# A decoder block with 16,384 single-neuron experts: one gather for each chosen expert, against every expert for every token with one-hot gates

## The reference, cut to what matters

```python
D_MODEL, SEQ = 1024, 1024                 # BATCH = 1, DEPTH = 1
N_KEYS, PEER_HEADS, PEER_TOPK = 128, 8, 16
N_EXPERTS = N_KEYS * N_KEYS

def reference(x, ...):
    h = rmsnorm(x, mix_norm_g)
    q, k, v, gb, gc, hc = split(h @ w_in, 6)
    mixed = concat(rmsnorm(stick_breaking_attention(q, k, v)),
                   rmsnorm(short_gated_conv(gb, gc, hc)))
    x = x + mixed @ w_out
    xn = rmsnorm(x, ffn_norm_g)
    x = x + peer(xn, peer_wq, peer_keys, peer_u, peer_v)
    return rmsnorm(x, final_norm_g)

def peer_chunk(xc, wq, keys, u_tab, v_tab):       # 128 tokens
    q = (xc @ wq).reshape(128, PEER_HEADS, 256)
    s1 = einsum('thd,hnd->thn', q[..., :128], keys[0])
    s2 = einsum('thd,hnd->thn', q[..., 128:], keys[1])
    v1, i1 = top_k(s1, 16); v2, i2 = top_k(s2, 16)
    best, pos = top_k(v1[..., :, None] + v2[..., None, :], 16)   # over 256 pairs
    idx = (i1 * N_KEYS + i2) at pos
    g = softmax(best)
    act = gelu(einsum('td,thkd->thk', xc, u_tab[idx]))
    return einsum('thk,thkd->td', g * act, v_tab[idx])
```

## Time and profile before

| | us |
|---|---|
| median of 3 runs | 3488.6 |
| range | 3485.1 to 3492.64 |
| the profiled execution | 3493.22 |
| its span, first to last instruction | 3491.5 |

### The profile page before, as it was taken

One profiled execution on the slowest core, in us unless ns is written; L12 is line 12 of the kernel. 1 busy time (PEld: TensorE's weight loads), 2 busy tenths in 40 slices (PEclk: granted clock), 3 DMA queues, 4 the chain that ended last, 5 costly groups with the idle time before them and its releaser, 6 DMA issues.

```text
span 3491.5 us, 29071 instructions
## 1 busy us (share of the span) xinstructions
PE 2454.5 (70%) x7552; PEld 1321.4 (38%) x7552; DVE 2663.4 (76%) x6520; ACT 687.7 (20%) x1947; POOL 1382.3 (40%) x1296
## 2 busy tenths in 40 slices
PE   8569895589989785675878787576667555554554
PEld 7447463246545342223544333243223222211221
DVE  1674689865778799897779788689877577777776
ACT  2122311121434111112114332111111111111111
POOL 0132323333334333444445445344444344444442
PEclk9779998899999897887889899898788777777777
DMA  6878697789888998889999999999888899999997
GB/s 217 313 299 325 266 381 292 292 334 356 331 330 329 380 355 311 325 339 368 415 411 377 341 370 388 387 394 371 334 356 340 337 374 380 380 370 372 380 383 293
DMA packets 185037, 1212.83 MB, mean 347 GB/s; under 512 B 20672, under 2 KB 20672, under 8 KB 53440
## 3 DMA queue, kind: packets, MB, share of 16 engines
q0 software_dynamic: 147456, 1073.81, 78.7%
q1 hardware_dynamic: 37440, 137.40, 10.4%
HBM read 1198.54 MB, written 12.58 MB: 347 GB/s over the span
## 4 chain that ended last, share of the span: by engine, by line
PE 34%; DVE 29%; DMA 23%; ACT 6%; issue 5%; POOL 2%; POOLq 0%; DVEq 0%; ACTq 0%; SPq 0%
DMA ring<-in_uv,cur_idx 22%; PE vacc L900 17%; DVE ring L1075 11%; PE bank L938 6%; DVE acc L1106 4%; ACT diag L731 3%; PE bank L1006 3%; PE o_ps L904 2%; POOL ring L694 2%; DMA xn<-in_final_norm_g 1%; PE bank L934 1%; DVE lt L1223 1%; DVE ocT L1233 1%; PE bank L949 1%; PE bank L967 1%
## 5 line engine op out<-in xcount | busy, mean ns | idle before, releaser
L900 PE MATMUL vacc<-ring,diag 128*128 128x512 f32 x2048 | 1267.1, 763 | 985.5 <-ACT diag L731 983.2
L694 POOL DMA_INDIRECT ring<-in_uv,cur_idx x1024 | 1215.1, 1187 | 1172.5 <-PE vacc L900 611.6
L1075 DVE CUSTOM_DVE_ANT_0 ring<-ring,xn 128x1024 f32<-128x1024 f32 x1024 | 1219.5, 1222 | 351.6 <-DMA ring<-in_uv,cur_idx 349.0
L900 PEld LDWEIGHTS vacc<-ring,diag 128*128 128x128 f32 x2048 | 481.7, 246 | 1670.2 <-ACT diag L731 1027.2
L1106 DVE SCALAR_TENSOR_TENSOR acc<-ring,g_w,acc 128x512 f32<-128x512 f32 x832 | 625.6, 752 | 35.2 <-DVE g_w L1098 0.6
L685 POOL COPY cur_idx<-idx 128x4 uint32<-128x4 uint32 (+1 forms) x256 | 165.2, 645 | 904.9 <-DVE acc L1106 693.6
L726 ACT ACTIVATE g_ex<-g_cu 128x4 f32<-128x4 f32 x256 | 52.4, 205 | 2071.6 <-DVE g_cu L1088 2055.3
L731 ACT ACTIVATE diag<-ident,g_w 128x128 f32<-128x128 f32 x1024 | 326.8, 390 | 187.8 <-DVE g_w L1098 184.5
L938 PE MATMUL bank<-hT,wpool 128*128 128x256 f32 (+2 forms) x1280 | 285.0, 382 | 1.4 <-ACT hT L757 1.4
L938 PEld LDWEIGHTS bank<-hT,wpool 128*128 128x128 f32 x1280 | 219.8, 192 | 69.1 <-issue 12.1
L1017 PE MATMUL bank<-hT,wpool 128*128 128x256 f32 (+2 forms) x1024 | 235.9, 386 | 0.7 <-ACT hT L839 0.7
(11 more groups left out here) (126 smaller groups left out, 1798.2 us busy)
## 6 DMA issues: line engine op xcount, KB each, us to landing
wpool<-in_w_in SPq DMA_DIRECT2D x96, 512.0 KB
wpool<-in_peer_wq SPq DMA_DIRECT2D x64, 512.0 KB
wpool<-in_w_out SPq DMA_DIRECT2D x32, 512.0 KB
ring<-in_uv,cur_idx POOLq DMA_INDIRECT x1024
xb<-in_x SPq DMA_DIRECT2D x15, 512.0 KB
x_scratch<-xb SPq DMA_DIRECT2D x8, 512.0 KB
xn_scratch<-xb SPq DMA_DIRECT2D x8, 512.0 KB
xn<-xn_scratch SPq DMA_DIRECT2D x8, 512.0 KB
```

The lines of the kernel that those rows point to most:

```text
L694: nc.gpsimd.indirect_dma_start(ring[:, s, :], None, uv, bass.IndirectOffsetOnAxis(ap=cur_idx[:, s:s + 1], axis=0))\
L900: ins = nc.tensor.matmul(vacc[:, :], diag[:, q, s, :], ring[:, q * GROUP + s, D:D + PE_COLS], start=first and s == 0, stop=last and s == G ...
L1075: ins = nc.vector.tensor_tensor_reduce(out=ring[:, s, 0:D], in0=ring[:, s, 0:D], in1=xn[:, c % 2, :], scale=1.0, scalar=0.0, op0=ALU.mult, ...
```

## The change

The front keeps its mathematics. The gathers, the ring and the body are gone. In their place all 16,384 experts are applied to all tokens, in 128 tiles of 128 experts (tile a holds the experts whose first key is a), and a **pass** over all tiles is made for each 256 tokens. That is 4 passes x 128 = 512 tiles.

- For one tile n, `up` is eight 128x256 products (L836), `down` four 128x512 products (L848) that accumulate in four PSUM banks over the pass.
- The gates of a tile (128 experts by 256 tokens) are zero but for the chosen experts. They are built by `scatter`: for each token, a 128x128 one-hot matrix of its slots' second keys (`one_b`, DVE L1105, bare ones) times a 128x64 matrix that holds the gate where the slot's first key matches (`one_a`, DVE L1113). Four tokens make a step (four products with a 64-wide moving tile, L824), 64 steps cover 64 first keys for 256 tokens (a range), and ACT copies them out of PSUM into `gates` (L638).
- The gates are built a range, 64 tiles, ahead: at tile n the step n+64 is made. The first 64 steps stand before tile 0, and the last 64 tiles have none.
- The gelu of a tile goes from ACT (Square, L656) to DVE (L1148) to ACT (Tanh, L658) to DVE (L1153), then DVE multiplies with the gates (L1160).
- Each tile loads 512 KB of u and 512 KB of v by plain DMAs of SP, with three slots for each.
- The front is in four batches of two chunks. `front_line()` lays the projections of one batch beside the attention of the batch before and the search of the one before that, in six rounds. The dense part starts when the whole front is over (`front_over`). Results of the search are transposed into `selT`.

The core of the diff (of the front only its order; all lines here are new, in place of `timeline`, of the groups and of `final_sum` and its like):

```diff
-BATCHES = [[0], [1, 2], [3, 4, 5], [6, 7]]
+BATCHES = [[0, 1], [2, 3], [4, 5], [6, 7]]
+PASSES = S // T
+TILES = PASSES * NKEYS
+RANGE = 64
+SCAT_TOK = T // RANGE
+USLOTS = 3
+VSLOTS = 3
+HBUF = 4
...
+def front_line():
+    out = []
+    for r in range(len(BATCHES) + 2):
+        lists = []
+        for stage, make in enumerate((proj_steps, mix_steps, find_steps)):
+            if 0 <= r - stage < len(BATCHES):
+                lists.append(make(r - stage))
+        marked = [((i + 0.5) / len(ls), n, i) for n, ls in enumerate(lists) for i in range(len(ls))]
+        for _, n, i in sorted(marked):
+            out += lists[n][i]
+    return out
...
+            front_over(sp)
+            for n in range(TILES):
+                if n >= USLOTS:
+                    sp.wait_ge(s_up, n - USLOTS + 1)
+                sp.dma_start(u_in[:, n % USLOTS, :], ut[n % NKEYS]).then_inc(s_uin[n % USLOTS], 16)
+                if n >= VSLOTS:
+                    sp.wait_ge(s_vp, n - VSLOTS + 1)
+                sp.dma_start(v_in[:, n % VSLOTS, :], vt[n % NKEYS]).then_inc(s_vin[n % VSLOTS], 16)
...
+            for n in range(TILES):
+                act.wait_ge(s_up, n + 1)
+                if n >= HBUF:
+                    act.wait_ge(s_vp, n - HBUF + 1)
+                nc.scalar.activation(hid[:, n % HBUF, :], u_ps[n % 2][:, 0:T], ACT.Square).then_inc(s_hsq, 1)
+                act.wait_ge(s_hcu, n + 1)
+                nc.scalar.activation(hid[:, n % HBUF, :], hid[:, n % HBUF, :], ACT.Tanh,
+                                     scale=GELU_TANH * GELU_CUBE).then_inc(s_hth, 1)
+                if n % 2 and n + RANGE < TILES:
+                    store_gates((n + RANGE) // 2)
...
+            def scatter(s):
+                q = s // 2
+                pe.wait_ge(s_one, s + 1)
+                if s % 2 == 0 and q >= 2:
+                    pe.wait_ge(s_gates, q - 1)
+                for j in range(SCAT_TOK):
+                    o = ((s % 2) * SCAT_TOK + j) * RANGE
+                    ins = nc.tensor.matmul(sc_ps[q % 2][:, o:o + RANGE], one_b[:, s % 2, j, :], one_a[:, s % 2, j, :],
+                                           start=True, stop=True, skip_group_check=True)
+                ins.then_inc(s_scat, 1)
...
+            def up(n):
...
+                pe.wait_ge(s_uin[n % USLOTS], 16 * (n // USLOTS + 1))
+                if n >= 2:
+                    pe.wait_ge(s_hgl, n - 1)
+                for k in range(KD):
+                    ins = nc.tensor.matmul(u_ps[n % 2][:, 0:T], u_in[:, n % USLOTS, k * P:(k + 1) * P],
+                                           xT[:, p % 2, k * T:(k + 1) * T], start=k == 0, stop=k == KD - 1)
+                ins.then_inc(s_up, 1)
+
+            def down(n):
...
+                pe.wait_ge(s_vin[n % VSLOTS], 16 * (n // VSLOTS + 1))
+                pe.wait_ge(s_hw, n + 1)
...
+            front_over(pe)
+            for s in range(RANGE):
+                scatter(s)
+            for n in range(TILES):
+                up(n)
+                if n + RANGE < TILES:
+                    scatter(n + RANGE)
+                if n > 0:
+                    down(n - 1)
+            down(TILES - 1)
...
+            for s in range(RANGE):
+                ones_b(s)
+                ones_a(s)
+            for n in range(TILES):
+                h = hid[:, n % HBUF, :]
+                u = u_ps[n % 2][:, 0:T]
+                r = n // RANGE
+                dve.wait_ge(s_hsq, n + 1)
+                nc.vector.scalar_tensor_tensor(out=h, in0=h, scalar=1.0 / GELU_CUBE, in1=u, op0=ALU.add,
+                                               op1=ALU.mult).then_inc(s_hcu, 1)
+                if n + RANGE < TILES:
+                    ones_b(n + RANGE)
+                dve.wait_ge(s_hth, n + 1)
+                nc.vector.scalar_tensor_tensor(out=h, in0=h, scalar=1.0, in1=u, op0=ALU.add, op1=ALU.mult)\
+                    .then_inc(s_hgl, 1)
+                if n + RANGE < TILES:
+                    ones_a(n + RANGE)
...
+                dve.wait_ge(s_hgl, n + 1)
+                nc.vector.tensor_tensor(h, h, gates[:, r % 2, n % RANGE, :], ALU.mult).then_inc(s_hw, 1)
```

More of the change, by code:

```diff
@@ L281, in bank_uses @@
     if name == "out_proj":
-        return [("out", *args, part) for part in range(2)]
+        return [("out", *args)]
     return []
@@ L289, in bank_frees @@
     if name == "store_xn":
-        return [("turn_xn", args[0], i) for i in range(2)]
+        return [("turn_xn", *args)]
     if name == "store_proj":
@@ L856, in front @@
                     c, = args
[L857 to L869 removed]
+                    u = ("turn_sel", c)
@@ new lines, in _, with store_gates @@
+            for eng, name, *args in line:
+                if eng == "act":
+                    front(name, args)
+            def store_gates(q):
+                r, t0 = divmod(q * 2 * SCAT_TOK, T)
+                act.wait_ge(s_scat, 2 * q + 2)
+                if t0 == 0 and r >= 2:
+                    act.wait_ge(s_hw, RANGE * (r - 1))
+                nc.scalar.activation(gates[:, r % 2, :, t0:t0 + 2 * SCAT_TOK],
+                                     sc_ps[q % 2][:, :].rearrange("p (t r) -> p r t", r=RANGE), ACT.Copy)\
+                    .then_inc(s_gates, 1)
@@ new lines, in final_root @@
+            def final_root(c):
+                p, i = divmod(c, 2)
+                act.wait_ge(s_y2, c + 1)
+                ss(nc.scalar.activation(x2[:, :], y_rows(p, i), ACT.Square, accum_out=st[:, 12:13]))
+                ss(nc.scalar.activation(st[:, 13:14], st[:, 12:13], ACT.Ln, bias=eps[:, 0:1], scale=1.0 / D))
+                nc.scalar.activation(st[:, 14 + i:15 + i], st[:, 13:14], ACT.Exp, scale=-0.5).then_inc(s_fsq, 1)
+            front_over(act)
+            for s in range(1, RANGE, 2):
+                store_gates(s // 2)
@@ L1032, in front @@
                     ins.then_inc(s_full, 1)
-            pe.wait_ge(s_pool, 8)
-            for c, first, count in gather_line(group, front, "pe"):
-                with pe.Fori(first, first + count) as i:
-                    for q in range(2):
-                        for part in range(PARTS):
-                            group(c, i, q, part, False, False)
+                elif name == "turn_sel":
+                    c, = args
+                    pe.wait_ge(s_exp, search_no[(c, PH - HS)])
+                    b = take(("turn_sel", c))
+                    for i in range(3):
+                        ins = nc.tensor.transpose(b[:, i * P:(i + 1) * P], sel[:, c % 2, i, :], ident[:, :])
+                    ins.then_inc(s_full, 1)
@@ L1100, in add_rows @@
-            def add_rows(c, G, q, first):
-                dve.wait_ge(s_gw, G + 1)
-                for k in range(GROUP):
-                    if not (first and c == 0 and k == 0):
-                        dve.wait_ge(s_vd, G * GROUP + k)
-                    s = q * GROUP + k
-                    nc.vector.scalar_tensor_tensor(out=acc[:, c % 2, PE_COLS:D], in0=ring[:, s, D + PE_COLS:2 * D],
-                                                   scalar=g_w[:, s:s + 1], in1=acc[:, c % 2, PE_COLS:D],
-                                                   op0=ALU.mult, op1=ALU.add).then_inc(s_vd, 1)
@@ L1336, in _ @@
[L1336 to L1344 removed]
+                    to = slice(h0 * TOPK, (h0 + HS) * TOPK)
```

1217 lines of the change are left out of this document (498 added, 719 removed).

## The result

| | before | after |
|---|---|---|
| median of 4 runs, us | 3488.1 | 7171.7 |
| range | 3485.1 to 3492.64 | 7165.43 to 7173.67 |
| the profiled execution | 3493.22 | 7172.09 |
| its span | 3491.5 | 7170.0 |

The changed kernel takes 2.056 times as long (95% interval 2.052 to 2.059). The forecast was 7070 us, in a range of 6300 to 7600.

A forecast was written before the change was run, and what follows sets the result against it. It took the kernel before as bound by a ring of eight slots whose makers wait for each other, gathers' transfers as floor. Front 1200, first scatters 100, tiles 5309 and 441, end 20 sum to 7070 us; range 6300 to 7600.

The forecast's parts named there:

- front: Projections, attention and search before the dense part: 1200 us, between 1069 and 1350, including 1011 us of TensorE work.
- first 64 scatter steps: Scatter steps before tile 0, bound by DVE at 0.65 + 0.85 us each: 96, plus 4 for first loads, 100 us.
- 448 tiles: Dense tiles with a scatter, 11.85 us each including wait and slow clock: 5309 us.
- 64 tiles: Last dense tiles, without a scatter, 6.89 us each: 441 us.
- end: Four copies, two residual sums, roots and scales, a load and the store: 20 us.
- The wait that the order makes: In each tile the scatter waits for one_a behind the same tile's gelu: 2.9 us after up, bounds 2.5 and 3.3.
- What a product costs: TensorE per tile at full clock: up 3.455, scatter 0.86, down 3.43, together 7.75 us.
- The clock: Dense tiles: idle TensorE makes 16 of 23 product bursts slow, adding 1.2 us a tile: 11.85 us.
- The rival in which the clock holds: Dense tiles wait as forecast but at full clock, 10.65 us each: 6530 us in all; chance 0.2.
- Not slower: Rival: dense tiles take 4.2 us each, perhaps by products at twice the pace (3320 us); chance 0.01.

The follow-up runs named there:

- Experiments 1 and 2: Two runs on the changed kernel: TensorE's scatter moved behind the down products (5505.4 us); or DVE's one-hot rows made ahead of the tile's gelu (5502.3 us).
- experiment 4: Changed kernel with four idle 256-column identity products between up and scatter in each of 448 tiles; 6856.8 us.
- experiment 3: Changed kernel with only the gated one-hot rows (one_a) made ahead of the gelu, the bare ones left in place; 6602.4 us.
- Experiment 6: Kernel with scatter behind the down products, plus ACT copying key scores into four SBUF buffers that DVE's search reads; 5458.9 us.
- experiment 8: Kernel with scatter behind down and key scores copied by ACT, plus bf16 operands for experts' products, converting loads, down two tiles behind; 3438.9 us.
- experiment 5: Kernel with only the gated rows ahead of the gelu, plus one idle 256-column product (0.43 us) before each tile's scatter; 6304.4 us.
- experiment 7: Kernel with scatter behind the down products, plus one idle 256-column product ahead of each of the first 64 scatter steps; 5562.2 us.
- experiment 9: The bf16 kernel with both one-hot rows made at the start of DVE's tile; 3121.0 us, 0.894 of the kernel before.

## Why the prediction was right, and where it was off

The direction, the mechanism of the dense part and the time hold: 7170.0 us of span against 7070. But the agreement within 100 us is partly luck, since an error of +225 us in the front and one of -149 us in the dense tiles offset each other.

| step | forecast, us | measured | difference |
|---|---|---|---|
| front | 1200 | 1425.2 | +225 |
| first 64 scatter steps | 100 | 116.5 | +17 |
| 448 tiles | 5309 | 5159.8 | -149 |
| 64 tiles | 441 | 444.4 | +3 |
| end | 20 | 24 | +4 |

- **The wait that the order makes: right.** From the moment at which another product could have started (3019.09 + 3.455 = 3022.545) to the scatter at 3025.46 are 2.915 us, against 2.9. The handover to ACT is 0.20 and the Square with its handover 0.42. From there the starts of DVE are 0.34, 0.60 and 0.33 apart, shorter than the durations taken, and `one_a` takes 0.98 where 0.85 was taken between 0.45 and 1.24. The Tanh, costed at nothing up to 0.6, took 0.42 and ended before DVE was through with `one_b`. Experiments 1 and 2 show that this wait is made by the order alone.
- **What a product costs: right.** `up` at 3.455 is exact. `down` is 3.49 (3.43), the scatter 0.94 (0.86); a tile at full clock is 10.80 us (10.65). The record with a new stationary tile and few columns, 0.107 us in the earlier trace rows, was the right price. By the issue gap that the Trainium skill gives (page "TensorE: Matmul & The Clock Gate", section "Back-to-back issue gap") the scatter would have been an estimated 0.2 us; for float32 the trace, with 0.94, does not agree.
- **The clock: the mechanism right, its size wrong.** I took the share of slow bursts from 23 irregular ones in the earlier trace rows, 16 of 23, and 1.2 us a tile. Of the 446 groups of down products whose records are complete 166 were slow, 37%; the cost is 11.52 - 10.80 = 0.72 us, and experiment 4 gives 0.70 by itself. This is the -149 us: 448 x (0.15 + 0.72 - 1.2). One reading in it was wrong too: that the slow bursts of the earlier trace rows start at the low clock. The one at 3231.51 does, as do five others, but the one at 369.28 has a granted clock of 1.00 in its first microsecond, and six others have over 0.9 there; the clock fell during them. In the changed kernel's dense part it fell 166 times, 140 of them 1.4 or 1.5 us behind the start of a scatter. The rival in which the clock holds was wrong: the clock fell behind 2.76 us and, in experiment 3, behind 1.53. The rule of the Trainium skill (same page, section "Why this matters for your kernels") warns only of longer idle gaps, and the trace does not agree with it.
- **The front: a term mis-sized, beyond its upper bound of 1350.** My sum had 1011 us of TensorE's work at full clock and 189 of waits and start. The first row of the stretches has 1122.81 us busy and 302 idle. So the excess is 112 us of busy time and 113 us of idle time. In the trace 166 us of the front's busy time lie at a granted clock of 0.50; at twice the full clock's price they account for at most 83 of the 112 us, by estimate. I had priced the low clock only in the dense part though the same kind of idle gaps stood in the front. What is left, some 30 us, lies in my prices of the products and was not traced further. The largest idle entry (148.7 us) stands at the one bank of key scores; I had looked for waits in the attention chain. Experiment 6 recovers 50 us by freeing the bank, and the rest of the difference is not settled run by run.
- **The first scatter steps: priced as bound by DVE, at 1.5 us a step.** At half clock TensorE's 1.71 us a step are more than DVE's 1.56, and the two wait for each other, 1.82 in all. With the cheap products of experiment 8, at the same clock of 0.50, the 64 steps take 94.2 us, close to the 96 that DVE alone was priced at.
- **Not slower.** It asked for 4.2 us a tile. It took products at twice the pace of the earlier trace rows, and they kept that pace: 3.455 us for `up`. Experiments 1 and 2, with next to nothing idle, stay at 7.8 us, 1.58 times the kernel before. With cheaper products it was reached, at 3.97 and 3.28 us.

## What to carry to other kernels

Work made far ahead is only ahead if the engines' orders let it be: ask of each instruction what stands before it in the order of its own engine, not only what it reads. A wait that runs through the orders of two engines can be opened in either. A wait that one stage hides comes back when that stage becomes cheaper, so look at the order again after every change of price. Where an engine stands idle in each round, its clock can be a second loss beside the wait (it was behind 1.53 and 2.76 us, and was not behind 1.03 and 1.10), to be priced everywhere that such gaps occur, the front included.

## What the runs showed of the hardware that I had not expected

- Idle products made the kernel faster: 0.43 us of them a tile 298 us (experiment 5), 1.7 us of them 315 us (experiment 4), by keeping the granted clock at 1.00.
- TensorE ran 116 us at a granted clock of 0.50 on narrow products, with some 0.1 us a step of waiting, and 163 us with a 256-wide product in each step (experiment 7). The clock was already 0.50 at the end of the front, where TensorE was mostly idle, and rose once wide products stood together: in the changed kernel `up(0)` starts at 1541.73, and the granted clock is 0.89 from 1545 to 1550 us. A busy engine is not yet a fast one; what sets the clock there was not settled.
- Eight float32 records with 64 moving columns take 0.94 us, 0.117 each; in bf16 four take 0.12 us, 0.03 each (2503.09 to 2503.21 in experiment 9). For bf16 the trace agrees nearly with the issue floor of about 25 ns of the Trainium skill (page "TensorE: Matmul & The Clock Gate", section "Back-to-back issue gap"). So the 64-wide scatter is nearly 8 times cheaper in bf16, and the 256-wide products 4 times (2503.21 to 2504.09, 0.88 us, against 3.455).
